# Scan units of a two-layer hybrid block: fixed PSUM banks, another order of VectorE's sums, and an earlier first unit

## The reference

```python
def ssd_scan(...):                       # per chunk, 6 heads
    seg = jnp.exp(jnp.where(causal, cum[..., :, None] - cum[..., None, :], -jnp.inf))
    scores = jnp.einsum('bclhn,bcshn->bchls', cc, bc) * seg
    y = jnp.einsum('bchls,bcshp->bclhp', scores, xdt)
    y = y + jnp.einsum('bclhn,bchpn->bclhp', cc, entering) * jnp.exp(cum)...

def mlstm_scan(...):
    s = jnp.einsum('bchld,bchsd->bchls', qc, kc) * jnp.exp(log_w - m_t[..., None])
    num = jnp.einsum('bchls,bchsv->bchlv', s, vc) + a_inter[..., None] * jnp.einsum('bchld,bchvd->bchlv', qc, c_in)
    hid = num / jnp.maximum(jnp.abs(den), jnp.exp(-m_t))[..., None]

y = y_f + flip(y_b) + xh * p['ssd_d'][:, None]
out = rmsnorm(y * jax.nn.silu(z), p['ssd_norm_w'])
out = jax.nn.sigmoid(o.astype(f32)) * h.reshape(b, L, MLSTM_WIDTH)
```

## Time and profile before

| | |
|---|---|
| median of 3 runs | 1482.56 us (1481.58 to 1483.47) |
| profiled execution: time | 1487.4 us |
| profiled execution: span | 1485.6 us |
| TensorE busy, of the span | 1207.9 us, 81% |
| VectorE busy | 616.6 us, 42% |
| ScalarE busy | 315.4 us, 21% |
| TensorE's mean granted clock | 0.895 |
| scan of layer 0, about | 302 to 435 us |
| scan units of layer 1, about | 1014 to 1108 us |

### The profile page before, as it was taken

The page is one execution under the profiler, slowest core; times in us unless marked ns, Lnnn a source line. Parts: engine busy times, 40 slices in busy tenths (PEclk is TensorE's granted clock), DMA queues, the critical chain, the costliest instruction groups (busy, mean ns, idle before and its releaser), DMA issues. The chain is left out here.

```text
span 1485.6 us, 19748 instructions
## 1 busy us (share of the span) xinstructions
PE 1207.9 (81%) x7632; PEld 796.4 (54%) x7632; DVE 616.6 (42%) x1222; ACT 315.4 (21%) x624; POOL 128.3 (9%) x144
## 2 busy tenths in 40 slices
PE   3899999988899479899757359999988498887880
PEld 1444548976679444454434246568767355444550
DVE  3434863036873632442212264844473522222223
ACT  2302012343342111131101122122522111111111
POOL 0000000000000022222112000000000122222210
PEclk9899999988799679999979779999979599999895
DMA  8633232335330559999989455341633399999982
GB/s 289 193 114 113 66 95 81 100 120 180 128 118 29 198 193 374 393 380 375 371 254 386 189 187 188 114 128 44 199 122 133 140 354 393 383 375 378 386 323 90
DMA packets 155173, 322.18 MB, mean 217 GB/s; under 512 B 28299, under 2 KB 111304, under 8 KB 138440
## 3 DMA queue, kind: packets, MB, share of 16 engines
q1 hardware_dynamic: 143688, 305.13, 57.2%
q0 software_dynamic: 11392, 15.77, 3.4%
HBM read 321.11 MB, written 21.23 MB: 230 GB/s over the span
## 5 line engine op out<-in xcount | busy, mean ns | idle before, releaser
L564 PE MATMUL bank<-hT,ring 128*128 128x512 f32 (+1 forms) x544 | 203.6, 531 | 1.9 <-DVEq L1164 1.1
L564 PE MATMUL bank<-ring,qkT 128*64 128x256 f32 x1024 | 166.5, 417 | 39.5 <-DMA ring<-in_moe_w_up 25.1
L564 PE MATMUL bank<-ring,hT 128*128 128x256 f32 (+1 forms) x928 | 179.0, 347 | 1.5 <-DVE ysum L1585 1.5
L1585 DVE TENSOR_TENSOR xbc<-xbc,bank 64x256 f32<-64x256 f32 x65 | 27.5, 423 | 333.7 <-ACT xbc L1246 300.8
L564 PEld LDWEIGHTS bank<-ring,hT 128*128 128x128 f32 x928 | 153.3, 193 | 19.9 <-issue 2.0
L564 PEld LDWEIGHTS bank<-hT,ring 128*128 128x128 f32 x544 | 102.4, 190 | 97.7 <-issue 91.5
L564 PEld LDWEIGHTS bank<-ring,qkT 128*64 128x64 f32 x1024 | 106.8, 150 | 70.1 <-issue 26.7
L564 PE MATMUL bank<-hT,qkT 128*64 128x256 f32 x512 | 100.4, 417 | 33.6 <-DMA hT<-in_moe_w_up 22.5
L1179 POOL DMA_INDIRECT pair_rows<-hyT,zotok x65 | 59.9, 922 | 449.5 <-DVE xbc L1591 424.9
L1246 ACT ACTIVATE xbc<-bank 64x256 f32<-64x256 f32 x65 | 24.6, 378 | 319.8 <-PE bank L564 319.8
L564 PEld LDWEIGHTS bank<-hT,qkT 128*64 128x64 f32 x512 | 59.4, 151 | 50.2 <-issue 28.4
(11 more groups left out here) (293 smaller groups left out, 1639.4 us busy)
## 6 DMA issues: line engine op xcount, KB each, us to landing
ring<-in_w_mod SPq DMA_DIRECT2D x40, 1024.0 KB, 7.7
ring<-in_moe_w_down SPq DMA_DIRECT2D x33, 1024.0 KB, 12.4
ring<-in_moe_w_gate SPq DMA_DIRECT2D x32, 1024.0 KB, 14.8
ring<-in_moe_w_up SPq DMA_DIRECT2D x32, 1024.0 KB, 10.6
ring<-in_w_in SPq DMA_DIRECT2D x22, 1024.0 KB, 5.5
hT<-in_moe_w_gate SPq DMA_DIRECT2D x16, 1024.0 KB, 14.1
hT<-in_moe_w_up SPq DMA_DIRECT2D x16, 1024.0 KB, 9.7
hT<-in_moe_w_down SPq DMA_DIRECT2D x16, 1024.0 KB, 12.0
```

Of the source, the lines that this page charges most:

```text
L564: return nc.tensor.matmul(o, a, b, start=s, stop=e, **k)
L1585: step(V.tensor_tensor(o, a, b, op), *names)
```

## The change

- `product` takes an optional bank. `occupant` keeps who has each bank; products without a bank take the next in turn, and only they move the turn on.
- In a unit: segment banks 0, 1 and 0 again, key-query products 2 and 3, `ys` 4, `carried` 5 and 6, `mn` 7, `st` 4. Modulations of a unit take banks 0, 1, 0; a `mod_vector` takes bank 1.
- `weights_of` makes segment banks 0 and 1, then the key-query products, then the third segment bank.
- Layer 0: `weights_of(0)` and `segments(0)` stand ahead of the last o tile on TensorE and ScalarE.
- VectorE: `combine` is split. The order of a unit is scores(u+1), SSD sums(u), prep(u+1), state(u), modulation columns, mLSTM sums(u), and then the gating work that stood ahead of prep (gated(0) at unit 5, gated(1) and normed(0) at unit 6 of layer 0; gated(3) to normed(3) at unit 7 of layer 1).
- TensorE, unit 7 of layer 0: `mixed(0)` behind the outputs of the unit.

```diff
-            def product(name):
-                n = len(products)
-                products.append(name)
-                at[("bank", name)] = n % BANKS
-                if n >= BANKS:
-                    old = products[n - BANKS]
+            def product(name, bank=None):
+                if bank is None:
+                    bank = turn[0] % BANKS
+                    turn[0] += 1
+                old = occupant.get(bank)
+                if old:
                     pe.wait_ge(*due(("read", old)))
...
+                occupant[bank] = name
+                at[("bank", name)] = bank
+                return banks[bank]
...
+                    segment_rows(0)
+                    segment_rows(1)
+                    both = [product(("qkcb", l, u, j), 2 + j) for j in range(2)]
...
+                    segment_rows(2)
...
                         if n == 2 * NT - 1:
                             decay_columns()
+                            pe.wait_ge(*due(("split", l)))
+                            pe.wait_ge(*due(("silu qk", l, 2)))
+                            weights_of(0)
                         token_major("zo"[n // NT], (n % NT,))
...
-                        b = product(("ys", l, u))
+                        b = product(("ys", l, u), 4)
...
-                            both = [product(("carried", l, u, j)) for j in range(2)]
+                            both = [product(("carried", l, u, j), 5 + j) for j in range(2)]
...
-                        b = product(("mn", l, u))
+                        b = product(("mn", l, u), 7)
...
-                        b = product(("st", l, u))
+                        b = product(("st", l, u), 4)
...
+                    outputs_of(u)
                     if (l, u) == (0, 7):
                         mixed(0)
-                    outputs_of(u)
...
-                            mod_vector(*vector)
-                    for part in mods_of_unit(l, u):
-                        modulation(*part)
+                            mod_vector(*vector, 1)
+                    for n, part in enumerate(mods_of_unit(l, u)):
+                        modulation(*part, n % 2)
...
                         if n == 2 * NT - 1:
                             decay_columns()
+                            segments(0)
                         (z_rows, o_rows)[n // NT](n % NT)
...
                 for u in range(len(units)):
                     if u < last_unit:
                         scores(u + 1)
+                    ssd_sums(u)
+                    if u < last_unit:
+                        prep(u + 1)
+                    next_state(u)
+                    if u:
+                        for vector in vectors_after(mods_of_unit(l, u - 1)):
+                            mod_columns(*vector)
+                    ml_sums(u)
                     if l == 0 and u == 5:
                         gated(0)
                         head_squares(0)
...
                         normed(3)
-                    if u < last_unit:
-                        prep(u + 1)
-                    combine(u)
```

More of the change, by code:

```diff
@@ L334, in slot_v @@
             return area.rearrange("p (k n) -> p k n", k=k)
-        products = []
+        occupant, turn = {}, [0]
         loads = []
@@ L572, in stage_end, with modulation @@
                 pe.wait_ge(*due(("end", "dve", l, stage)))
-            def modulation(l, n):
-                b = product(("mod", l, n))
+            def modulation(l, n, bank=None):
+                b = product(("mod", l, n), bank)
                 pe.wait_ge(*due(("load", ("mod", l, n))))
@@ L582, in modulation, with mod_vector @@
                 last.then_inc(pe_done, made(("mod", l, n), ("used", ("mod", l, n))))
-            def mod_vector(l, m):
-                b = product(("modc", l, m))
+            def mod_vector(l, m, bank=None):
+                b = product(("modc", l, m), bank)
                 pe.wait_ge(*due(("modrow", l, 4 * m + 3)))
@@ L808, in decay_columns, with weights_of, segment_rows @@
                     mm(b[:, :], ones[:, :], MX).then_inc(pe_done, made(("dcb", l)))
+                units = [(i, d, i if d == 0 else BACK[i]) for i in range(NT) for d in range(2)]
+                def weights_of(u):
+                    i, d, c = units[u]
+                    if c < t0:
+                        return
+                    ck = slice(c * P, (c + 1) * P)
+                    def segment_rows(n):
+                        b = product(("w", l, u, n), n % 2)
+                        mm(b[:, :], ident16[:, :], mask_v[:, d:d + 1, :].broadcast_to([P, 4, P]), True, False)
+                        for i4 in range(4):
+                            m, h = (4 * n + i4) // 6, (4 * n + i4) % 6
+                            last = mm(b[:, i4 * P:(i4 + 1) * P], trio_v[:, 2 * m + d, h:h + 1].broadcast_to([P, P]), RL16[:, ck],
+                                      False, i4 == 3)
+                        last.then_inc(pe_done, made(("w", l, u, n)))
+                    segment_rows(0)
+                    segment_rows(1)
+                    both = [product(("qkcb", l, u, j), 2 + j) for j in range(2)]
+                    for q in range(4):
+                        for j in range(2):
+                            keys, queries = (qk_v[64 * j:64 * j + 64, 3 + q, ck], qk_v[64 * j:64 * j + 64, q, ck]) if q < 3 else \
+                                (xbc_v[64 * j:64 * j + 64, 3, ck], xbc_v[64 * j:64 * j + 64, 4, ck])
+                            last = mm(both[j][:, q * P:(q + 1) * P], keys, queries)
+                            if q == 3:
+                                last.then_inc(pe_done, made(("qkcb", l, u, j)))
+                    segment_rows(2)
                 for q in range(3):
@@ L841, in _ @@
                     decay_columns()
[L843 to L867, removed]
                 def mixed(t):
@@ L1434, in segments @@
                                *names, bias=cols_v[:, c, 3, 64 * m + 32 * d + h:64 * m + 32 * d + h + 1])
+                part_after()
+                scan_rows()
+                for t in range(2):
+                    v_rows(t)
+                if l == 0:
+                    for t in range(2, NT):
+                        v_rows(t)
+                    for n in range(2 * NT):
+                        if n < NT:
+                            tokens(n)
+                        else:
+                            scan_columns(n - NT)
+                        if n == 2 * NT - 1:
+                            decay_columns()
+                            segments(0)
+                        (z_rows, o_rows)[n // NT](n % NT)
+                else:
+                    for c in range(2):
+                        tokens(c)
+                    for c in range(NT):
+                        scan_columns(c)
+                    decay_columns()
                 def gated_squares(t):
@@ L1460, in _ @@
                 order = MIX_ORDER[l]
-                segments(0)
+                if l:
+                    segments(0)
                 for u in range(len(units)):
@@ L1973, in combine, with ml_sums @@
                             tt(y3, y3, nds_v[:, :, 0, :, 0:HD], ADD)
+                def ml_sums(u):
+                    i, d, c = units[u]
+                    if c >= t0:
                         dve.wait_ge(*due(("made", ("mn", l, u))))
@@ L1993, in combine, with next_state @@
                         written.add(("h", c))
+                def next_state(u):
+                    i, d, c = units[u]
                     if i < NT - 1:
```

34 lines of the change are left out of this document (5 added, 29 removed).

## The result

The changed kernel is slower: 1491.35 us median (1488.16 to 1493.79) against 1483.01 (1481.58 to 1483.88), ratio 1.0056, 95% interval 1.0034 to 1.0078. A repetition gives 1.0060 (1.0042 to 1.0077). The forecast was 1484.4.

The account below looks back on a forecast made before the run. No engine alone but the loop between TensorE, VectorE and ScalarE was taken to bound the scan units. Profiled 1487.4 - 4.1 (layer 0) + 6.0 (layer 1) = 1489.3 us, less 4.8 gives a median of 1484.4; range 1475 to 1491.

Parts of the forecast that it names:

- third bank's wait: Layer 0, unit 1: its third segment bank waits for ScalarE's exponentials, so TensorE idles 3.0 us ahead of ys(0).
- st's in unit 1: Layer 0, unit 1: st shares bank 4 with ys and waits from 334.5 for VectorE's scores(2) till 335.65.
- the second modulation's: Layer 0, unit 3: behind a modulation vector the second modulation waits 1.3 us until VectorE is past the state update.
- TensorE idle behind the square: Layer 0, ahead of unit 7's first bank: modulation copies stand behind ScalarE's square of gated(0); TensorE idle 6.9 us.
- normed(1) ahead of the earlier trace: End of layer 0: normed(1), the tail's start on VectorE, begins at 414.7 instead of 418.81, so layer 0 gains 4.1 us.
- the walk: Layer 0 worked out unit by unit, at 2.4 GHz from unit 1 on, unit 6 at half clock; sum -4.1 us.
- half clock in layer 0 too: Rival, chance 0.25: idles in units 1 and 3 drop the clock behind unit 3; layer 0 gains only 0.6, 1488.0 us.
- half clock through unit 4: Layer 1: idles of 1.5 and 1.65 us bring half clock in unit 4's carried, mn, st and modulations; layer 1 +6.0 us.
- full-clock case: Rival, chance 0.27: layer 1's waits don't bring 1.2 GHz; layer 1 only +0.3 us, 1478.8 us.
- the three waits: Layer 1: unit 4's third bank 2.9 us, unit 5's first bank 1.5 for a modulation's copy, its third bank 1.65.
- The change does what it says: Rival, chance 0.10: ScalarE not late, VectorE's 10.2 us set each unit; layer 0 gains some 10 us, layer 1 nothing, 1473 us.
- those two waits: Kernel before, layer 0: unit 4's key-query products wait 1.27 us for mLSTM sums, ys(3) 1.76 for the state update; fixed banks remove both.

Follow-up runs that it names:

- e_last: Changed kernel with gated(3) to normed(3) of layer 1 ahead of unit 7's sums again; 1.0007 of the kernel before.
- e_act: Changed kernel with ScalarE copying a unit's modulations ahead of the square, root or mixed tile that stood before them; 1.0058 of the kernel before.
- e_rr: Changed kernel with all products taking banks in turn as before, engine orders unchanged; 0.9942 of the kernel before, median 1474.1 us.
- e_best: Changed kernel with banks in turn, gated(3) ahead of the last sums, square of gated(0) behind unit 7's exponentials; 0.9886 of the kernel before, median 1466.5 us.
- e_order: Kernel before with VectorE's new order alone, no fixed banks, old product order and first unit behind the last o tile; 1.0030 of the kernel before.
- e_rr_w: Changed kernel with banks in turn and the third segment bank ahead of the key-query products again; 0.9942 of the kernel before.
- e_rr_last: Changed kernel with banks in turn and gated(3) to normed(3) ahead of unit 7's sums in layer 1; 0.9887 of the kernel before.

## Why the prediction was wrong

**Layer 0, -4.1 forecast, -2.3 found.** Most steps came as written: third bank's wait 3.0 us (2.83), st's in unit 1 1.15 (1.16), the second modulation's 1.3 (1.22), TensorE idle behind the square 6.9 us (6.61), ys(0) with half clock behind it, normed(1) ahead of the earlier trace rows. From the decay product on, normed(1) starts 2.4 us earlier than before, 1.7 less than I summed. Behind the decay product ys(0), ys(2) and ys(3) come within 0.3 us of the walk (15.9, 42.1 and 51.5 forecast; 15.6, 42.2 and 51.8 found), but ys(1) came 2.0 us early (30.65 forecast, 28.6 found), for half clock ended before unit 0's modulations did, and half clock in unit 1's modulations (3.64 us instead of 1.9) took it back: the agreement at ys(2) and ys(3) is two errors that cancel, so luck. The term that was mis-sized is the clock: I had 2.4 GHz from unit 1 on, and it fell behind the two modulation vectors, at 332 and at 359. The second made ys(4) 1.5 us late, and half clock already in unit 7's segments, which I had begun only with ys(6), made ys(6) 3.2 us late. The rival "half clock in layer 0 too" named the mechanism, its place too late and its price (3.5 us) too high.

**Layer 1, +6.0 forecast, +5.6 found, by another way: that the number fits is luck.** I took half clock through unit 4, for 5.7 us; the granted clock stayed full from 1015 to 1097, so this step failed (window of the changed kernel, columns as above).

```profile
1015.00:1097.00 82.00, 69.65 (x671) 58.03 (x670) 40.50 (x81) 31.87 (x70) 1.10 (x2) 1.00 0.51 163
```

My full-clock case gave +0.3. It took the three waits that it had (2.9, 1.5 and 1.65 us) for more than they measured (1.47, 1.34, 1.47), and it missed two others: products without a bank of their own now meet the fixed ones, 1.60 us for a token tile behind the state's bank and 1.92 us ahead of unit 4's first segment bank behind a sigmoid (no row of before shows them, but the order of the text did). A third part is no effect of the change at all: the v tiles ran at half clock for a while (12.99 us instead of 10.83), in both traces of the changed kernel and in the kernel before with VectorE's order alone, but not in e_last's or e_act's. The moved gating was sized rightly: 4.8 us of it, by the run that puts it back. Behind the decay product of layer 1 the traces show three parts, us:

| | ys(4) | ys(7) | output projection |
|---|---|---|---|
| before | 45.8 | 86.1 | 95.9 |
| changed | 56.7 | 83.6 | 101.3 |
| banks in turn (e_rr) | 45.6 | 79.7 | 98.9 |
| fastest (e_best) | 45.1 | 79.2 | 92.1 |

So the 11 us that the changed kernel loses ahead of ys(4), some 2 of them the clock's, are gone with banks in turn; from ys(4) to ys(7) it then takes 26.9 us instead of 40.3, at full clock where before had 0.54 and 0.59 (1070 to 1080, 1090 to 1100); and the gating behind ys(7) takes 8 us of that away again.

**The sum.** The step that failed most is the last one: 1489.3 us for a profiled execution, less 4.8, was taken for the median of the changed kernel. Its profiled execution took 1488.2 us, near the forecast, but it is the fastest of its four and lies 3.2 us below their median (4.2 in the repetition), while that of before, 1487.4, lies above all its other runs. In terms of the sum: +1.9 us forecast, +3.3 found in the two scans, +8.3 between the medians. A stage's difference, measured twice, was near; that it would be the difference of the medians nothing had shown, and 5 us of that are still not explained. The range ended at 1491.0, the median is 1491.35: it had no room for this.

**The rivals.** "The change does what it says" named the gain it could have, 10 us in layer 0, and "against it speaks ScalarE's queue". That was close: with banks in turn the orders give 11 to 16. What I didn't see is that the *banks*, which I had read as the part that takes waits away, are what withholds it. My argument for them was the earlier trace rows; but those two waits were made by the late mLSTM sums and the late state. With VectorE's new order and no fixed bank the second is gone, and the first stays at 1.41 us (e_order) or 1.40 (e_rr_w), where layer 0 still takes only 119.6; with the third segment bank behind the key-query products it is 0.25 (e_rr).

**Table loads and short idles.** The drain that the Trainium skill (ScalarE: Activation LUTs, What ACT_TABLE_LOAD costs) adds to a table load isn't seen here either: in the changed kernel the sigmoid ends at 310.62, a load starts at 310.64 and the first exponential at 311.94, 1.30 us. The remark of the Trainium skill on short idles between groups of matmuls that make the clock swing as a kernel cycles through banks (TensorE: Matmul & The Clock Gate, A second HAM failure mode: psum-queue depth-cycling) is neither borne out nor refuted. Banks in turn has the fewest idles, and its clock was full till 378 in one execution (e_rr) but fell at 322 in one of the same code (e_rr_last), behind the same wait of 2.59 us; the changed kernel, which has more waits, fell at 315 and at 332.

## What to carry to other kernels

A fixed bank is a second use that must wait for the first one's reader, and that reader's queue comes along with it: before banks are fixed, name for each pair that shares one the engine that frees it and what stands ahead of that read. Here ys and st on one bank, and two segment banks on another, tied TensorE to VectorE and ScalarE just where the head start was to let it run ahead. When one lock is taken off and the time stays, look at the next product in the text for the wait that was behind it. And where work is moved behind sums that another layer's critical chain needs (gated(3) here), give each layer its own order.

## What the runs showed of the hardware

The granted clock made up to 5.5 us in one stage between executions of the same instructions: 118.8 us at full clock up to 378, 124.3 with half clock from 322 for 14 us (the second one's window, columns as above). A wait of 2.59 us on TensorE stood ahead in both. A change to the scan that moves less than this can't be judged from one trace each.

```profile
322.00:336.00 14.00, 14.00 (x119) 10.74 (x118) 6.85 (x15) 2.28 (x7) 0.00 (x0) 0.52 0.43 142
```
